# A four-layer network in one kernel: raw tokens turned first, and a new order in attention, stages' first products, a level loop and the last norms

## The reference, cut to what matters

```python
def hybrid_layer(x, p_i, ...):                 # first block, two layers
    proj = rmsnorm(x, g_pre_mix) @ w_in
    # a: attention over selected keys, b: forgetting, c: differential, d: window with sinks
    x = x + rmsnorm(concatenate([o_a, o_b, o_c, o_d]) @ w_out, g_post_mix)
    h = rmsnorm(x, g_pre_mlp)
    x = x + rmsnorm(square(relu(h @ w_up)) @ w_down, g_post_mlp)
    return x + sigmoid(x @ w_ple_gate) * (p_i @ w_ple_proj)

def second_block(x, ...):                      # two layers
    for layer in range(2):
        mix = token_mixer(x, ...)              # gMLP gate, gated deltanet (chunks of 64), dilated attention, @ w_out
        x = layer_norm(DN_ALPHA * x + mix, ln1_g, ln1_b)
        f = swiglu(x, ...) if layer == 0 else moe_swiglu(x, ...)   # 8 experts, 2 per token
        x = layer_norm(DN_ALPHA * x + f, ln2_g, ln2_b)
    return x
```

## Time and profile before

| | before |
|---|---|
| median of 3 runs | 2036.7 us (2036.54 to 2036.83) |
| the profiled execution, its own time | 2037.11 us |
| its span in the trace | 2035.2 us |
| granted TensorE clock, mean | 0.997 |
| PE, DVE, ACT, POOL busy | 1989.1, 1584.5, 1210.4, 96.9 us |
| bytes read from HBM | 478.00 MB |

### The profile page before, as it was taken

The page is one execution under the profiler, slowest core; times in us unless marked ns, Lnnn a source line. Parts: engine busy times, 40 slices in busy tenths (PEclk is TensorE's granted clock), DMA queues, the critical chain, the costliest instruction groups (busy, mean ns, idle before and its releaser), DMA issues.

```text
span 2035.2 us, 30362 instructions
## 1 busy us (share of the span) xinstructions
PE 1989.1 (98%) x11719; PEld 1682.0 (83%) x11719; DVE 1584.5 (78%) x1636; ACT 1210.4 (59%) x1293; POOL 96.9 (5%) x162
## 2 busy tenths in 40 slices
PE   8999999999999999999999999999999999999996
PEld 7778888877888888888889888888888888888885
DVE  7777754777775469785448978989999998999998
ACT  5565534556553456544335645777777777777774
POOL 0310000031000000000000000000000000000000
PEclk9999999999999999999999999999999999999998
DMA  8316555531655554155546308999999999999994
GB/s 295 129 53 206 195 194 192 201 123 60 202 188 196 194 193 151 38 192 186 186 162 212 125 2 322 357 364 368 360 368 363 359 368 361 367 362 365 367 361 179
DMA packets 154216, 481.58 MB, mean 237 GB/s; under 512 B 14616, under 2 KB 41728, under 8 KB 153984
## 3 DMA queue, kind: packets, MB, share of 16 engines
q1 hardware_dynamic: 150048, 465.45, 63.5%
q0 software_dynamic: 4064, 14.68, 2.1%
HBM read 478.00 MB, written 2.10 MB: 236 GB/s over the span
## 4 chain that ended last, share of the span: by engine, by line
PE 91%; DVE 5%; ACT 2%; DMA 1%; issue 1%; POOL 0%; SPq 0%; DVEq 0%
PE G L664 19%; PE G L666 18%; PE G L665 18%; PE Sp L664 5%; PE Sp L666 5%; PE Sp L665 5%; PE G L1102 3%; PE G L691 3%; PE G L1103 2%; PE G L660 1%; DVE ring_lo L2059 1%; PE Sp L1102 1%; PE G L1480 1%; PE G L655 1%; DMA ring<-in_w_in 1%; PE G L656 1%
## 5 line engine op out<-in xcount | busy, mean ns | idle before, releaser
L1987 ACT ACTIVATE e_hi<-e_raw 128x1408 fp32r<-128x1408 f32 x384 | 523.5, 1380 | 155.0 <-DMA e_raw<-in_moe_w_gate 58.3
L2808 DVE TENSOR_TENSOR e_lo<-e_raw,e_hi 128x1408 fp32r<-128x1408 f32 x384 | 601.2, 1619 | 18.6 <-ACT e_hi L1987 16.5
L2059 DVE TENSOR_TENSOR ring_lo<-ring,ring_hi 128x2048 fp32r<-128x2048 f32 (+2 forms) x171 | 383.4, 2253 | 190.8 <-ACT ring_hi L1567 189.5
L1567 ACT ACTIVATE ring_hi<-ring 128x2048 fp32r<-128x2048 f32 (+1 forms) x179 | 335.4, 1882 | 236.3 <-PE G L666 173.6
L664 PE MATMUL G<-e_hi,xgTh 128*128 128x512 f32 (+1 forms) x768 | 291.8, 380 | 0.0
L666 PE MATMUL G<-e_hi,xgTl 128*128 128x512 f32 (+1 forms) x768 | 288.3, 375 | 0.0
L665 PE MATMUL G<-e_lo,xgTh 128*128 128x512 f32 (+1 forms) x768 | 285.4, 372 | 0.0
L664 PE MATMUL G<-ring_hi,xT 128*128 128x512 f32 (+2 forms) x544 | 213.0, 391 | 0.0
L666 PE MATMUL G<-ring_hi,xT 128*128 128x512 f32 (+2 forms) x544 | 209.3, 385 | 0.0
L665 PE MATMUL G<-ring_lo,xT 128*128 128x512 f32 (+2 forms) x544 | 209.0, 384 | 0.0
L666 PEld LDWEIGHTS G<-e_hi,xgTl 128*128 128x128 f32 x768 | 144.0, 188 | 25.1
(11 more groups left out here) (427 smaller groups left out, 3278.3 us busy)
## 6 DMA issues: line engine op xcount, KB each, us to landing
e_raw<-in_moe_w_gate SPq DMA_DIRECT2D x128, 704.0 KB, 5.9
e_raw<-in_moe_w_up SPq DMA_DIRECT2D x128, 704.0 KB, 6.0
e_raw<-in_moe_w_down SPq DMA_DIRECT2D x128, 704.0 KB, 5.9
ring<-in_w_in SPq DMA_DIRECT2D x48, 1024.0 KB, 5.1
ring<-in_w_mlp_up SPq DMA_DIRECT2D x32, 1024.0 KB, 5.2
ring<-in_w_mlp_down SPq DMA_DIRECT2D x32, 1024.0 KB, 4.8
ring<-in_w_out SPq DMA_DIRECT2D x16, 1024.0 KB, 4.9
ring<-in_ffn_w_gate SPq DMA_DIRECT2D x22, 512.0 KB, 3.8
```

The lines of the kernel that those rows point to most:

```text
L1567: nc.scalar.activation(ring_hi[:, n % H, 0:m], ring[:, n % R, 0:m], ACT.Copy).then_inc(w_hi.sem, 1)
L1987: nc.scalar.activation(e_hi[:, u, :], e_raw[:, u, :], ACT.Copy).then_inc(w_hi.sem, 1)
L2059: v.tensor_tensor(ring_lo[:, n % R, cs], ring[:, n % R, cs], ring_hi[:, n % H, cs].bitcast(F32), ALU.subtract).then_inc(w_lo.sem, 1)
L2808: v.tensor_tensor(e_lo[:, u, :], e_raw[:, u, :], e_hi[:, u, :].bitcast(F32), ALU.subtract).then_inc(w_lo.sem, 1)
```

## The change

Eight things are changed.

1. **Start.** The raw tokens are turned. The gain is loaded as 8 rows of 128, turned by PE into a column, and multiplied in by DVE while it reads the turned tokens from PSUM (`gained`). 1/rms is applied later, as the scale of ACT's copies of the projection (`columns_taken`). The second block of tokens and the positions are loaded behind the first four weight tiles, the post-mix gain too; the angles are made behind the splits of the first four weights.
2. **Attention.** An `Exp` of one number (`warm`) stands between two earlier copies. ACT takes the turned probabilities of unit 0 before a copy of columns, and `exps(3)` moves one unit later. Turned outputs and the `c` heads of block 1 go to `Sp[:, 0, :]` in place of `T[0]`. `values` waits only until the probabilities are taken. A half of `out_rows(1, 0)` stands ahead of `output_transposes(0, 0)`. `CHOOSE_AT` changes.
3. **End of the first block.** DVE takes the turned high columns (`block_evac(0)`) between two splits, and not behind both.
4. **`lead`.** The products of block 1 with the first weight tile are cut in two. Those with the high part of the tokens (8 matmuls, by both parts of the weight) stand ahead of the remaining `low(j)` of block 0, behind a wait for the high part alone; those with the low part of the tokens stay in the old place.
5. **Levels.** The turn into `T[0]` of levels 1 to 3 stands before the second products of its level, and not behind them.
6. **FFN.** The last chunk goes to `Sp`, and a wait for the chunk's result goes.
7. **Last product and routing.** `last_product` makes block 1 by halves of the columns, so that DVE adds and sums the first half before the second is there; the routing of block 1 is cut finer.
8. **Last norm.** The sums are added by halves; ACT takes mean and squares, DVE centres and finishes into `XN`.

```diff
@@ sync, start
-        sp.dma_start(POS[:, :], w["positions"][0]...)
-        for tb in range(NTB):
-            sp.dma_start(X[:, tb, :], w["x"][0, tb * P:(tb + 1) * P, :]).then_inc(x_loaded[tb].sem, 16)
+        sp.dma_start(GAIN8, w["norm_pre_mix"][0].rearrange("(k p) -> k p", p=P)).then_inc(gain_loaded.sem, 16)
+        sp.dma_start(X[:, 0, :], w["x"][0, 0:P, :]).then_inc(x_loaded[0].sem, 16)
         for n, use in enumerate(TILES):
+            if n == LEAD:
+                sp.dma_start(X[:, 1, :], w["x"][0, P:S, :]).then_inc(x_loaded[1].sem, 16)
+                sp.dma_start(POS[:, :], w["positions"][0]...)
...
@@ PE, lead
             high(3)
+            banks_free(banks_of(0, 1))
+            pe.wait_ge(x_hi[0].sem, n_x[0])
+            part(slots[0], 0, 1, range(4), product_of_high_tokens)
             for j in range(ahead, 3):
                 last = low(j)
...
-                    last = part(slots[j], j, 1, range(4), product)
+                    last = part(slots[j], j, 1, range(4), product if j else product_of_low_tokens)
...
@@ PE, attention
                 if u == 5:
+                    out_rows(1, 0, range(2))
                     output_transposes(0, 0)
-                    out_rows(1, 0)
+                    out_rows(1, 0, range(2, 4))
...
-                values(u)
+                values(u, probs_taken)
                 if u == 2:
                     last_columns(2, 1)
-                    rotated_transposes(QK_C, 1, c_rotated)
-                    bank_free_t(0)
+                    pe.wait_ge(g_act.sem, G_ACT * l + 2 * IN_N - 1)
+                    kept = t_free[0]
+                    rotated_transposes(QK_C, 1, c_rotated, Sp[:, 0, :])
+                    c_taken, t_free[0] = t_free[0], kept
...
@@ PE, levels
                 if lv >= LEVELS - 2:
                     dilated_logits(lv - (LEVELS - 2))
+                elif lv <= NTB:
+                    tb = lv - 1
+                    transposes(0, [(T[0][:, h * P:(h + 1) * P], CV[:, 4 + h, tb * P:(tb + 1) * P]) for h in range(H2)])
+                else:
+                    gate_transposes(0)
                 for tb in range(NTB):
                     pe.wait_ge(d2pe.sem, d2pe.next("pe"))
...
@@ ACT, attention
             heads_evac(QKT[:, QK_C:QK_C + 4, 0:P])
+            nc.scalar.activation(warm[:, l:l + 1], c("one"), ACT.Exp)
             heads_evac(QKT[:, QK_D:QK_D + 4, 0:P])
             exps(0)
             exps(1)
-            act.wait_ge(w_used.sem, n_use["act"] + 2)
-            columns_taken(5, 1, Sp[:, 0, :])
...
@@ DVE, start
+        def gained(tb):
+            for i in range(2):
+                dve.wait_ge(x_full[i].sem, n_x[i] + 1)
+                v.tensor_tensor(scaled_of(tb, i), T[i][:, :].rearrange("p (k s) -> p k s", k=4),
+                                GAIN_T[:, 4 * i:4 * i + 4].unsqueeze(2).to_broadcast([P, 4, P]), ALU.mult).then_inc(x_scaled[i].sem, 1)
...
@@ DVE, end of the first block
+                met(0, 1)
+                block_evac(0)
                 met(0, 2)
-                block_evac(0)
...
@@ ACT, last norm
+        for tb in range(NTB):
+            act.wait_ge(f_sum.sem, 2 * tb + 2)
+            nc.scalar.activation(ar(2 * FT2 * S + tb * HALF, D), ACC[:, tb, :], ACT.Identity, scale=-1.0 / D, accum_out=mv[:, tb, 0:1]).then_inc(f_mean.sem, 1)
+            act.wait_ge(f_mean.sem, tb + 1)
+            nc.scalar.activation(ar(2 * FT2 * S + tb * HALF, D), ACC[:, tb, :], ACT.Square, bias=mv[:, tb, 0:1], accum_out=mv[:, tb, 1:2]).then_inc(f_sq.sem, 1)
```

More of the change, by code:

```diff
@@ L611, in half_bank @@
     def half_bank(tb, half):
-        return G[:, 1, :] if tb == 1 and half == 1 else T[0]
+        return T[0] if half == 0 else G[:, 1, :] if tb else Sp[:, 0, :]
     HIGH_AT = (2, 3, 5, 6)
@@ L705, in token_transposes, with cols_tile @@
                 transposes(i, [(T[i][:, k * P:(k + 1) * P], src[:, tb, (4 * i + k) * P:(4 * i + k + 1) * P]) for k in range(4)], parts=True)
-        def cols_tile(slots, j, tb, width, bank, groups=range(4), product=product):
+        def cols_tile(slots, j, tb, width, bank, groups=range(4), product=product, dst=G):
             bh, bl = slot_cols_of(ring_hi, slots[0], width), slot_cols_of(ring_lo, slots[1], width)
@@ L711, in cols_tile @@
             for k in groups:
-                last = product(G[:, bank, 0:width], xTh[:, 4 * j + k, toks], xTl[:, 4 * j + k, toks], bh[:, k, :], bl[:, k, :],
+                last = product(dst[:, bank, 0:width], xTh[:, 4 * j + k, toks], xTl[:, 4 * j + k, toks], bh[:, k, :], bl[:, k, :],
                                j == 0 and k == 0, j == 1 and k == 3)
@@ L830, in product_rows, with last_product, part @@
             tokens_made(by)
+        def last_product(src, ready, by, tail):
+            def part(slots, j, tb, groups, product):
+                return rows_tile(slots, 2, xTh, xTl, 2 * j, KT, tb, g_of(tb), groups, product)
+            slots = []
+            bank_free_t(0)
+            banks_free([0, 1])
+            for j in range(LEAD):
+                if j == 2:
+                    bank_free_t(1)
+                slots.append(weights_high())
+                part(slots[j], j, 0, range(4), product_high)
+                if j == 2:
+                    weights_low(slots[0])
+                    part(slots[0], 0, 0, range(4), product_low)
+                    token_transposes(src, 1, ready)
+            for j in range(1, LEAD):
+                weights_low(slots[j])
+                last = part(slots[j], j, 0, range(4), product_low)
+            last.then_inc(g_half.sem, 1)
+            bank_free_t(0)
+            bank_free_t(1)
+            banks_free([2, 3])
+            for h in range(2):
+                for j in range(LEAD):
+                    if h and j == 1:
+                        tail()
+                    last = part(slots[j], j, 1, (h, h + 2), product)
+                    if h:
+                        last.then_inc(w_used.sem, 1)
+                if h == 0:
+                    last.then_inc(g_quarter.sem, 1)
+            tokens_made(by)
         def product_tokens(src, ready, by, tail, after_first=None):
@@ L867, in head_transposes, with rotated_transposes @@
                            act_takes=i == 0)
-            def rotated_transposes(first, tb, s):
+            def rotated_transposes(first, tb, s, bank=None):
                 pe.wait_ge(s.sem, NTB * l + tb + 1)
-                transposes(0, [(T[0][:, k * P:(k + 1) * P], head_source(first + k, tb)) for k in range(4)], act_takes=True)
+                dst = T[0] if bank is None else bank
+                transposes(0, [(dst[:, k * P:(k + 1) * P], head_source(first + k, tb)) for k in range(4)], act_takes=True, other=bank is not None)
             def index_dots(r):
@@ L996, in output_transposes @@
                 bank = half_bank(tb, half)
-                other = tb == 1 and half == 1
+                other = half == 1
                 kept = t_free[0]
```

213 lines of the change are left out of this document (137 added, 76 removed).

## The result

The changed kernel takes 2047.2 us (median of 8 runs, 2041.8 to 2050.7); the kernel before took 2037.3 us in the 8 runs beside it. The ratio is 1.0043, 95% interval 1.0035 to 1.0052. The prediction of 2023.1 us, faster, was wrong. The profiled execution of the changed kernel took 2048.72 us, its span is 2046.9. Three executions with a mean clock of 0.56 to 0.90 (one of e1 at 3305.8 us, two of the kernel before at 2482.0 and 2116.9 us) are slow from end to end and are left out of every number.

A forecast was written before the change was run, and what follows sets the result against it. PE, 91% of what ended last, was taken as the bound, so only its waits counted. Eight terms summed to -13.6 us from the profiled 2037.1: 2023.5, or 2023.1 for the median; range 2015.5 to 2030.5.

The forecast's parts named there:

- 1 start: Kernel start: first product 3.8 us earlier, 1.1 given back by DVE; -2.7 us, bounds -3.9 and -0.5.
- 2 attention: Attention of two layers: seven PE waits each cured, about four fifths kept as DVE is next; -9.0 us, bounds -12 and -4.
- 3 end of first block: Second block's first product: the 0.96 us wait for the tokens' low part goes; -1.1 us, bounds -1.1 and 0.
- 4 lead: Stages beginning with `lead`: eight matmuls give DVE time for the first low part; -2.1 us, bounds -2.6 and +1.
- 5 levels: Mixer levels 2 and 3: turn waits for DVE, +1.9 us each; level 1 -0.25; +7.2 in all, bounds +8 and -1.8.
- 6 FFN: FFN groups: the 1.0 us wait ahead of the last chunk's products goes; -1.1 us, bounds -1.1 and 0.
- 7 last product: Last product and routing: 2.8 us earlier, but experts' weights come no earlier; -1.2 us, bounds -2.8 and 0.
- 8 last norm: Last norm: work DVE did alone is shared with ACT and POOL; -3.6 us, bounds -4.2 and -2.
- Rival C: `lead`: new wait for block 1's high tokens, up to 1.9 us in each of ten stages; slower, 2044 us; chance 0.02.
- Rival A: Levels: PE finds `T[0]` free or the shift is taken up; -1 instead of +7.2, 2014.9 us; chance 0.16.

The follow-up runs named there:

- e1: The changed kernel with the turns of the levels back in their old place, all else kept: 2021.8 us, ratio 0.9915.
- e5: e1 with DVE's copy of the convolution's columns ahead of a weight split and the post-mix gain loaded five tiles later: 2018.3 us, ratio 0.9902.
- e4: e1 with all edits of the start undone too: 2020.0 us, ratio 0.9905.
- e6: e4 with the attention edits undone too: 2027.8 us, ratio 0.9946.
- e2: The kernel before with only the early turns of the levels added: 2059.7 us, ratio 1.0091.
- e7: e4 with the `lead` edits undone too: 2023.2 us, ratio 0.9922.
- e8: e4 with the edits of last product, routing and last norm undone too: 2026.2 us, ratio 0.9938.
- e3: The changed kernel with 18 unread turns ahead of the waiting turn in levels 2 and 3: 2032.2 us, ratio 0.9966.
- e9: e5 with the turn into `T[0]` ahead of the second products in level 1 alone: 2018.0 us, ratio 0.9900.

## Why the prediction was wrong

| part | forecast | measured | from |
|---|---|---|---|
| 1 start | -2.7 | +1.8, within noise (-1.3 to -1.6 when mended) | e1, e5 against e4 |
| 2 attention | -9.0 | -7.9 (-7.2 by the stamps) | e6 |
| 3 end of first block | -1.1 | -1.3 | stamps |
| 4 lead | -2.1 | -3.2 | e7 |
| 5 levels | +7.2 | +19 to +26 | e2; changed kernel against e1 |
| 6 FFN | -1.1 | -1.3 | stamps |
| 7 last product | -1.2 | -1.5 to -2.4 | stamps of e4, e7 and e8 |
| 8 last norm | -3.6 | -3.0 | last product to end of span |

**The step that failed is the fifth.** It found the wait, its place and its reason, and priced the wait alone: "+1.9" in four levels, measured 2.05 each as a wait and 8 to 10 us in all (e3 against e1). It put the clock at nothing without a reason: it did not ask what PE's clock does when PE, which in the levels runs mostly products of 64x64, stands for 2 us. The granted clock went to 0.50, and PE's work in the levels and the chain of states behind them took up to twice as long: another 16 to 18 us. Of the 24.1 us by which the forecast missed, some 19 are this step. No rival had the clock in it, and the term's upper bound of +8 was made from waits alone. The trace before could have raised the question, not answered it. Between the start and the last products no wait of PE was over 1.1 us, so a clock of 1.00 in those stages said nothing about a wait of 2. A wait of 2.54 in the start left the clock at 1.00, a wait of 1.61 at 2019.14 too; behind the last product, where PE has nothing more to do, it was at 0.50 within 3 us (the windows of the kernel before above). So the price of part 5 was open to both sides, and the bound of +8 needed a run. The same page of the Trainium skill, section "HAM oscillation — how this bites in real kernels", says that waits between short stretches of products can throttle TensorE again and again. Its example has waits for DMA of about 3 to 5 us, longer than any in the levels, so it does not by itself forecast this fall; the levels of the changed kernel show the pattern with waits of 2.05 us for DVE, 0.73 and 0.67 in the windows. The prediction did not weigh it.

**The first step failed too, by size.** The lead of the first product was right (-3.4; -3.8 forecast). What was taken for a give-back of 1.1 was at least all of it: the weights from 25 us on set the pace, and DVE's list, not changed behind the start, kept its old order. The bound of -0.5 excluded a loss without a reason.

**What held.** The other six terms are forecast at -18.1 and measured at -19.2 in e4 against its own kernel before. That they agree to 1.1 is in part luck, since attention won 1.1 to 1.8 less than forecast and `lead` 1.1 more. Attention was near the right size, with DVE as what comes next; the last norm won 0.6 less than forecast. ACT's passes and POOL and the last half rows of DVE follow one another like this in the changed kernel.

```profile
2037.64 1.28 DVE L3013 SCALAR_TENSOR_TENSOR XN<-ARENA,SM,VEC 128x1024 f32<-128x1024 f32 x1
...
2043.06 1.41 DVE L3016 SCALAR_TENSOR_TENSOR XN<-XN,SM,VEC 128x512 f32<-128x512 f32 x2 [0.79 <-POOL SM L3040]
...
2036.32 1.06 ACT L2135 ACTIVATE ARENA<-ARENA 128x1024 f32<-128x1024 f32 x1 [3.21 <-DVE ARENA L3008]
...
2039.82 1.15 ACT L2137 ACTIVATE ARENA<-ARENA,SM 128x1024 f32<-128x1024 f32 x1
...
2041.15 1.17 POOL L3192 TENSOR_SCALAR SM<-SM 128x1 f32<-128x1 f32 x1 [1.47 <-ACT ARENA L2137]
```

DVE ends at 2044.47, 8.5 us after PE's last product; before it was 11.5. ACT ends 5.1 us after that product, as forecast. But from there to DVE's last half rows it takes 2.0 us, where the forecast had 1.0 and two hops of 0.15: the scaling on POOL (L3192) took 1.17, and 0.19 for the first block of tokens. Why the second is longer was not traced, and a span on POOL is rough.

Rival C (a new wait in `lead`) named the right sign for the wrong reason: no such wait was seen. Rival A (no cost in the levels, 2014.9) was wrong in its mechanism, as the waits of 2.05 us show; that e5 and e9, with the levels put back, come within 3 us of its number says nothing for it.

## What to carry to other kernels

Price an added PE wait twice: the wait, and what the clock does behind it. Two waits of 2 us in a stage of small products cost 4 to 5 us a stage by themselves and some 8 more in clock; unread products in the same waits gave the 8 back. Whether a given wait brings a fall could not be read from its length here (2.54 us without, 1.96 with), so such a change is measured, and the granted clock behind each wait looked at, before it is kept. And a transfer or a step that starts earlier only moves the end if everything that is fetched and copied behind it is moved along: compare stamps of the same instruction stage by stage, not the first one.

## What the runs showed that was not expected

A kernel can get 15 us faster by 72 unread products (e3 against the changed kernel; 18 in each of four waits). With half as many it was as fast (2030.2 and 2032.2 us). The fall of the clock lasts beyond its cause: in the first mixer it began 0.6 us after the wait ended and lasted to 829, while PE was at work until 828.6. It came back as PE stood in the next wait of 2.05 (ended at 830.63; 0.66 us for 16 second products at 831.22), fell again at 832.3 and stayed low to 846, with no wait of PE in between. In the second mixer it did not come back between the two waits. And its size varies between executions: 2041.8 us with a mean clock of 0.991 to 2050.7 with 0.985 for the changed kernel, 2019.6 to 2020.6 for e4, whose levels have no fall.
